# Loading each 2 MB weight chunk as two 1 MB transfers, each with its own semaphore, in a two-layer hybrid decoder step on one core

## The reference, cut to what matters

```
layer 0: x += hgrn2(rmsnorm(x))            # w_in 1024x4096, w_out 1024x1024, recurrence over 256 tokens
         x += (silu(x@w1) * (x@w3)) @ w2   # dense SwiGLU, hidden width 3584
layer 1: x += short_conv(rmsnorm(x))       # w_in 1024x3072, w_out 1024x1024
         x += sum over the top 2 of 8 experts of gate_e * swiglu_e(rmsnorm(x))   # each 1024 -> 3584 -> 1024
y = rmsnorm(x)
```

## Time and profile before

| | us |
|---|---|
| median of 3 runs | 1656.01 (1655.55 to 1657.95) |
| the profiled execution | 1652.16 |
| its span in the trace | 1650.3 |

### The profile page before, as it was taken

One profiled execution on the slowest core, in us unless ns is written; L12 is line 12 of the kernel. 1 busy time (PEld: TensorE's weight loads), 2 busy tenths in 40 slices (PEclk: granted clock), 3 DMA queues, 4 the chain that ended last, 5 costly groups with the idle time before them and its releaser, 6 DMA issues.

```text
span 1650.3 us, 22587 instructions
## 1 busy us (share of the span) xinstructions
PE 1554.6 (94%) x8758; PEld 1358.1 (82%) x8759; DVE 1255.2 (76%) x940; ACT 924.5 (56%) x645; POOL 36.4 (2%) x44
## 2 busy tenths in 40 slices
PE   6988889999997997999999999999999999999992
PEld 6987779999997997788878888888788788888872
DVE  5994457566566775888888888888888888888883
ACT  4421125343433335767777777767777667777771
POOL 0002010000000002000000000000000000000001
PEclk9997669999998998999999999999999999999997
DMA  7535235878872553999999999999999999999982
GB/s 246 192 103 160 58 103 197 314 265 310 317 249 84 213 206 130 388 363 377 377 373 369 380 388 369 367 370 355 388 375 358 376 380 374 367 369 379 364 300 93
DMA packets 209624, 484.46 MB, mean 294 GB/s; under 512 B 5498, under 2 KB 23002, under 8 KB 206508
## 3 DMA queue, kind: packets, MB, share of 16 engines
q1 hardware_dynamic: 205768, 473.66, 78.5%
q10 hardware_dynamic: 2532, 5.84, 0.9%
q0 software_dynamic: 1280, 4.33, 0.7%
HBM read 446.45 MB, written 37.40 MB: 293 GB/s over the span
## 4 chain that ended last, share of the span: by engine, by line
PE 51%; DMA 20%; DVE 15%; issue 7%; ACT 6%; ACTq 0%; POOL 0%; DVEq 0%; SPq 0%; POOLq 0%
DMA raw<-in_moe_w 19%; PE Q L1915 9%; PE Q L1565 8%; PE Q L1566 8%; PE Q L1567 8%; DVE wlo L880 7%; PE Q L1871 5%; PE Q L1869 5%; PE Q L1870 5%; ACT whi L747 4%; PE Q L1678 1%; DVE htl L1483 1%; DVE pb L1078 1%; PE Q L1651 1%; DVE pb L991 1%
## 5 line engine op out<-in xcount | busy, mean ns | idle before, releaser
L880 DVE TENSOR_TENSOR wlo<-raw,whi 128x2048 fp32r<-128x2048 f32 x414 | 940.5, 2289 | 223.6 <-ACT whi L747 135.8
L747 ACT ACTIVATE whi<-raw 128x2048 fp32r<-128x2048 f32 x336 | 635.0, 1916 | 265.7 <-DMA raw<-in_moe_w 226.3
L1869 PE MATMUL Q<-whi,xgh 128*128 128x512 f32 x896 | 357.7, 399 | 2.5 <-issue 2.4
L1871 PE MATMUL Q<-whi,xgl 128*128 128x512 f32 x896 | 353.7, 395 | 0.0
L1870 PE MATMUL Q<-wlo,xgh 128*128 128x512 f32 x896 | 352.7, 394 | 0.0
L1565 PE MATMUL Q<-xh,whi 128*128 128x264 f32 x1024 | 298.1, 291 | 20.4 <-DVEq L1047 8.0
L1566 PE MATMUL Q<-xl,whi 128*128 128x264 f32 x1024 | 296.5, 290 | 0.0
L1567 PE MATMUL Q<-xh,wlo 128*128 128x264 f32 x1024 | 295.0, 288 | 0.0
L1565 PEld LDWEIGHTS Q<-xh,whi 128*128 128x128 f32 x1024 | 198.4, 194 | 22.3 <-issue 11.8
L1869 PEld LDWEIGHTS Q<-whi,xgh 128*128 128x128 f32 x896 | 169.1, 189 | 39.4 <-issue 3.6
L1871 PEld LDWEIGHTS Q<-whi,xgl 128*128 128x128 f32 x896 | 169.0, 189 | 37.8
(11 more groups left out here) (229 smaller groups left out, 1165.0 us busy)
## 6 DMA issues: line engine op xcount, KB each, us to landing
raw<-in_moe_w SPq DMA_DIRECT2D x168, 2048.0 KB, 9.9
raw<-in_ffn_w SPq DMA_DIRECT2D x21, 2048.0 KB, 9.0
raw<-in_hgrn_w_in SPq DMA_DIRECT2D x8, 2048.0 KB, 8.4
xg_rows<-zeros SPq DMA_DIRECT2D x6, 2048.0 KB, 13.1
y_rows<-zeros SPq DMA_DIRECT2D x6, 2048.0 KB, 13.6
raw<-in_conv_w_in SPq DMA_DIRECT2D x6, 2048.0 KB, 8.3
raw<-in_hgrn_w_out SPq DMA_DIRECT2D x2, 2048.0 KB, 8.5
st<-in_state_hgrn SPq DMA_DIRECT2D x8, 512.0 KB, 5.4
```

Of the source, the lines that this page charges most:

```text
L747: a.activation(bufs(q)[0], raw[:, n % RAW, PW * (q % 2):PW * (q % 2 + 1)], ACT.Copy).then_inc(hi_done, 1)
L880: v.tensor_tensor(low, raw[:, slot, PW * half:PW * (half + 1)], high.bitcast(F32), ALU.subtract).then_inc(lo_done, 1)
L1869: t_.matmul(out, xgh[:, kt, :], high[:, w], start=(kt == 0), stop=False)
L1871: mm = t_.matmul(out, xgl[:, kt, :], high[:, w], start=False, stop=(kt == DT - 1))
```

## The change

The load of a chunk becomes two transfers of 1 MB, each of half the chunk's row groups, which is exactly one piece. Each half waits for the low split of the piece that lay there before (`n*2 - 5` for the first, `n*2 - 4` for the second), and each slot has two semaphores. ACT waits for the one of the half that it copies. To have semaphores left for that, those of the three RMSNorms' intermediate steps are merged into `squares_added` and `norm_rooted`, which count on over the norms.

```diff
+    NORMS = ["mix0", "ffn0", "mix1"]
...
-        raw_loaded = [sem(f"raw_loaded{i}") for i in range(RAW)]
+        raw_loaded = [[sem(f"raw_loaded{i}_{half}") for half in range(2)] for i in range(RAW)]
...
-                if not isinstance(n, int) or n >= RAW:
-                    sp.wait_ge(lo_done, n * 2 - (2 * RAW - 2))
                 k, w = src.shape[1], src.shape[2]
                 dst = raw[:, slot, :].rearrange("p (k w) -> p k w", k=k)
-                sp.dma_start(dst, src).then_inc(raw_loaded[slot], 16)
+                for half in range(2):
+                    if not isinstance(n, int) or n >= RAW:
+                        sp.wait_ge(lo_done, n * 2 - (2 * RAW - 1 - half))
+                    ks = slice(k // 2 * half, k // 2 * (half + 1))
+                    sp.dma_start(dst[:, ks, :], src[:, ks, :]).then_inc(raw_loaded[slot][half], 16)
...
-                    act.wait_ge(raw_loaded[slot], 16 * n3)
+                    act.wait_ge(raw_loaded[slot][half], 16 * n3)
...
-                             scale=1.0 / D).then_inc(sem("rs_" + which), 1)
+                             scale=1.0 / D).then_inc(sem("norm_rooted"), 1)
...
-                act.wait_ge(raw_loaded[n % RAW], (reg + (n // RAW + 1)) * 16)
+                act.wait_ge(raw_loaded[n % RAW][base % 2], (reg + (n // RAW + 1)) * 16)
...
-                    act.wait_ge(raw_loaded[n % RAW], loads * 16)
+                    act.wait_ge(raw_loaded[n % RAW][q % 2], loads * 16)
...
-                                AX.X, ALU.add).then_inc(sem("sr_" + which), 1)
+                                AX.X, ALU.add).then_inc(sem("squares_added"), 1)
...
-                dve.wait_ge(sem("rs_" + which), 1)
+                dve.wait_ge(sem("norm_rooted"), NORMS.index(which) + 1)
...
-                pe.wait_ge(sem("sr_" + which), 2)
+                pe.wait_ge(sem("squares_added"), 2 * NORMS.index(which) + 2)
```

## The result

The changed kernel took 1645.1 us (median of 6 runs, 1643.46 to 1645.58), the kernel before 1654.53 us in the same comparison (6 runs, 1650.65 to 1657.95). The ratio is 0.9938 (95% interval 0.9918 to 0.9958). The profiled execution took 1645.03 us with a span of 1643.3 us; the span is 7.0 us shorter than before.

What follows compares the result with a forecast made beforehand. The prediction took PE to bound the experts at 17.05 us a block, with DMA following. Its terms, 1.8 + 4.2 = 6.0 us less, took the median of 1656.01 to 1650.0 us, 0.36% faster; range 1646.5 to 1657.5 us.

Steps and rivals of the forecast that it cites:

- The stall at the first expert's start: First expert's start: PE's 1.80 us wait on `hx`, ending at 670.13 us, goes entirely; 1.8 us saved, zero as other bound.
- The stalls at w2: Start of w2 in the experts: earlier first pieces remove 4.2 of PE's 4.6 us of waits for `wlo`.
- What stays: Experts: 2.3 us of `htl` waits and the issue gaps depend on ACT and DVE order, not data; nothing gained.
- the added transfers: All chunk loads, 207 more transfers, 168 in the experts: cost to the DMA engines put at 0 in the sum.
- SP's issue: On SP: 0.75 us of issuing for a chunk, hidden in the 5.7 us that PE takes for one.
- rival B: Experts: smaller transfers cost DMA engine time; at 0.5 us each, 20 us over 56 blocks, 1676 us; chance 0.07.
- The signs in the experts: Experts: `wlo` waits 4.6 to under 1 us, `hx` wait gone, block 17.05 us, ACT's waits shift from DMA to PE.
- upper bound of 7.6: Experts: most that could be saved, 5.8 us at w2 plus 1.8 us at the first expert's start.
- The step from the profiled execution to the median: Whole kernel: profiled 1652.16 us lies 3.85 us below the median 1656.01, so forecast 1646.2 us becomes 1650.0 from the median.

Runs made afterwards that it cites:

- the repeat: The changed kernel run once more with no edit: 1643.7 us, ratio 0.9951 to the kernel before.

## Why the prediction was right or wrong

The way was right, and the size was not. The step that failed is the gain in the experts: the terms "The stall at the first expert's start", "The stalls at w2" and "What stays" make 1.8 + 4.2 + 0 = 6.0 us, and the two traces have 2.3 + 6.6 = 8.9 us. Of the 2.9 us between them, 1.9 us lie at w2 groups whose late start is listed as issue gaps of the weight load alone, and these stood in "What stays", which was put at nothing, as due to the order on ACT and DVE and not to data.

**Right.** The bound: PE at 17.05 us a block with DMA following it. Six executions of five ways to load, and one with half the bytes, all came to 934.27 us. Right too: the wait for `hx` at 668 us went (1.80 us before; PE has no wait there now, its weight load one of 0.5 us); the earlier stages gave nothing; the added transfers cost nothing that can be measured (four in place of one cost nothing either), so SP's issue and rival B were weighed rightly. The signs in the experts came as named: waits for `wlo` under 1 us, 17.05 us, ACT's waits for data down and those for PE up. The sign that the stages before 600 us stay as long failed in the profiled execution, by the 2.0 us of lower clock, and held in the repeat.

**Wrong: "What stays".** I left the 2.3 us for `htl` and the 3.3 us of issue gaps of the weight load, as the order's. With early data all of them went from this stretch. (One wait of 1.4 us for `htl` at the very end is in both kernels; it lies behind 1612 us in the kernel before.) The waits for `htl` are seen mostly at the same w2 groups as those for `wlo`: DVE has `htl` between two low splits, so a low split that waits for data makes `htl` late as well. The issue gaps stand at other groups that start late, without any wait for `wlo`. The experiment with half the bytes shows that of this loss the order causes none.

**"The stalls at w2", by the distances.** I took 4.2 us from a row of 4.6 us in six waits. The distances at those six waits, with the one behind each, are 4.0 us too long, so for these the term was near. The other 2.5 us of the 6.6 are in distances where no wait for `wlo` is listed: 1.9 us where the weight load has gaps listed as issue, and 0.6 us where nothing is listed, since the lists leave out waits under 0.15 us. Measuring the distance of like instructions finds them. With the 2.3 us of the head the expert stage lost 8.9 us in all, where I had 6.0 and an upper bound of 7.6.

**The step from the profiled execution to the median.** The miss in the median is 4.9 us: 3.4 us because the gain was 9.4 and not 6.0, and 1.5 us because the base of 1656.01 was a median of three runs, which came to 1654.53 with six. The prediction also carried the 3.85 us between the profiled execution and that median over as if they belonged to both kernels. The experiments speak against it. Four traces with 2 MB transfers and the normal issue have sums of 937.4, 939.0, 940.9 and 943.6 us and lose 7.1, 8.7, 8.9 and 13.6 us with the head; the changed kernel lost nothing in either trace. The runs say it too: in the comparison those of the kernel before spread over 7.3 us, those of the changed kernel over 2.1 us. So a part of the spread before is stalls, and they go as a whole, however many an execution has. For the profiled execution it adds up: 1652.16 - 8.9 = 1643.3 us, and with the 2.0 us of lower clock 1645.3, against 1645.03 measured. That the median of the changed kernel, 1645.1, lies as near is in part luck: the lower clock is seen in one trace, the repeat's median was 1643.7, and what separates the two medians no run shows.

**The rule of the Trainium skill.** "DMA: Bandwidth & Descriptors", section "Measured (HBM→SBUF, 128 partitions, SWDGE, issued from GpSimd)", gives 341 GB/s for 1 MB, and by it the experts would be an estimated 79 us longer. This case disagrees: 369 GB/s with 1 MB (655 to 1612 us) and 371 GB/s with 512 KB transfers (700 to 1600 us), both the rate that PE asks for, with more than one transfer in flight. What these could reach without PE's limit no run here shows.

**What stays open.** Why a lateness that is steady at ACT reaches PE in one block and not in another was not followed up. The small gain of the 1 MB transfers with coarse waits is at the edge of its interval, and its cause was not looked for. How long the round of a slot is, part by part, was not measured; that it stands at the edge is read from what the delays did.

## What to carry to other kernels

Where the bound engine's repeated unit has a clean length, take that as a candidate for the floor, and measure the distances between like instructions. In this kernel all that they had above the floor was late data, whatever the rows of waits called it, and a run with half the bytes showed it. Then the forecast is the floor, not the median less a saving. Where a stream of loads follows the bound engine through a few slots, a wait of the engine in between for data that is long in total but hardly reaches the bound engine can mean that the round of a slot has little slack. Delay the loads by one step to see it: here one low split, 2.3 us, cost 84 us (1736.6 less 1652.9). Freeing, refilling and awaiting a chunk by the size at which it is consumed moved this kernel off that edge at no cost in bandwidth; cutting the transfers without the finer waits did not.

## What was not expected of the hardware

Transfers of 512 KB kept up a stream of 371 GB/s over 900 us, with 672 transfers in the experts and no wait for data; their price for the DMA engines is an estimated 0.15 us each at most. Beside 371 GB/s of loads the 55 distances add up to what they do beside 189 GB/s, to 0.01 us. In four traces a wait of PE of 2.0 to 2.4 us at the first expert's start was followed by a stretch at the lower clock level (0.83 granted from 670 to 680 us) that cost another 1.6 us or so; after waits of 1.8 us and less it was not. In one trace of the changed kernel the lower level held longer on small matmuls (0.66 and not 0.89 from 130 to 145 us) and moved all that follows by about 2 us.
